# A convolution layer: GpSimd's diagonals behind the boundary's residual in short pieces, and a weight slab split during the taps

## The reference

```python
for i in range(DEPTH):
    kind, j = i % N_MIXERS, i // N_MIXERS
    a = rms_norm(h, mix_norm_pre[i])
    if kind == 0:
        m = dilated_attention_mixer(a, positions, attn_w_qkv[j], attn_w_o[j])
    elif kind == 1:
        m = short_conv_mixer(a, sc_w_in[j], sc_w_conv[j], sc_w_out[j])
    else:
        m = conformer_conv_mixer(a, cc_w_pw1[j], cc_b_pw1[j], cc_w_dw[j], cc_b_dw[j],
                                 cc_ln_g[j], cc_ln_b[j], cc_w_pw2[j], cc_b_pw2[j])
    h = h + rms_norm(m, mix_norm_post[i])
    f = conv_ffn(rms_norm(h, ffn_norm_pre[i]), ffn_w_in[i], ffn_w_conv[i], ffn_w_out[i])
    h = h + rms_norm(f, ffn_norm_post[i])
```

```python
def conformer_conv_mixer(x, w_pw1, b_pw1, w_dw, b_dw, ln_g, ln_b, w_pw2, b_pw2):
    a, g = jnp.split(x @ w_pw1 + b_pw1, 2, axis=-1)
    h = a * jax.nn.sigmoid(g)
    h = causal_dwconv(h, w_dw) + b_dw
    h = jax.nn.silu(layer_norm(h, ln_g, ln_b))
    return h @ w_pw2 + b_pw2
```

## Time and profile before

| | |
|---|---|
| median of 3 runs | 2284.12 us (2284.03 to 2288.83) |
| profiled execution | 2280.8 us, span of its profile 2278.9 us |
| PE busy | 2190.1 us |
| DVE busy | 1516.2 us |
| ACT busy | 1010.2 us |
| POOL busy | 461.5 us |
| end of layer 1's FFN on PE | 816.35 us |
| taps of layer 2 on PE | 884.25 to 925.9 us |
| output projection of layer 2 | 938.44 to 967.34 us |

### The profile page before, as it was taken

The page is one execution under the profiler, slowest core; times in us unless marked ns, Lnnn a source line. Parts: engine busy times, 40 slices in busy tenths (PEclk is TensorE's granted clock), DMA queues, the critical chain, the costliest instruction groups (busy, mean ns, idle before and its releaser), DMA issues.

```text
span 2278.9 us, 43583 instructions
## 1 busy us (share of the span) xinstructions
PE 2190.1 (96%) x16355; PEld 2004.7 (88%) x16355; DVE 1516.2 (67%) x2436; ACT 1010.2 (44%) x1355; POOL 461.5 (20%) x492
## 2 busy tenths in 40 slices
PE   6999999999999989999999999999999999989999
PEld 5998779978899868699889987799789999869999
DVE  6874868847688577388578848688465545645553
ACT  4334555534455433455443345555353342444342
POOL 2220005500145140035212200055013200100330
PEclk9999999999999989999999999999999999899999
DMA  5555135555545543245555551355545556103554
GB/s 170 184 184 184 38 127 175 185 192 165 192 163 185 178 130 121 69 162 184 180 167 187 185 190 41 109 177 184 190 153 166 175 175 189 43 1 130 184 187 145
DMA packets 299894, 350.28 MB, mean 154 GB/s; under 512 B 7494, under 2 KB 254940, under 8 KB 299804
## 3 DMA queue, kind: packets, MB, share of 16 engines
q1 hardware_dynamic: 298082, 347.07, 46.0%
q10 hardware_dynamic: 1466, 1.80, 0.2%
q0 software_dynamic: 256, 0.17, 0.0%
HBM read 346.34 MB, written 2.68 MB: 153 GB/s over the span
## 4 chain that ended last, share of the span: by engine, by line
PE 85%; DVE 9%; ACT 4%; issue 1%; DMA 1%; SPq 0%; ACTq 0%; DVEq 0%
PE ps L1980 25%; PE ps L1982 25%; PE ps L1981 24%; DVE w_lo L1461 3%; ACT w_hi L1092 2%; PE ps L2310 2%; PE ps L2281 1%; PE ps L2257 1%; DVE res L1583 1%; PE ps L2268 1%; DVE scaled_out L1577 1%; DVE a_lo L1487 1%; PE ps L930 1%; PE ps L2251 1%; DVE hstat L1520 1%
## 5 line engine op out<-in xcount | busy, mean ns | idle before, releaser
L1461 DVE TENSOR_TENSOR w_lo<-raw,w_hi 128x2048 fp32r<-128x2048 f32 (+2 forms) x328 | 744.4, 2270 | 534.4 <-ACT w_hi L1092 534.4
L1980 PE MATMUL ps<-a_hi,w_hi 128*128 128x256 f32 (+1 forms) x3352 | 953.5, 284 | 15.5 <-DVE a_lo L1487 7.6
L1981 PE MATMUL ps<-a_lo,w_hi 128*128 128x256 f32 (+1 forms) x3352 | 948.3, 283 | 0.0
L1982 PE MATMUL ps<-a_hi,w_lo 128*128 128x256 f32 (+1 forms) x3352 | 948.1, 283 | 0.0
L1092 ACT CAST w_hi<-raw 128x2048 fp32r<-128x2048 f32 (+2 forms) x328 | 613.4, 1871 | 626.7 <-PE ps L1982 603.7
L1980 PEld LDWEIGHTS ps<-a_hi,w_hi 128*128 128x128 f32 x3352 | 635.4, 190 | 20.3 <-DVE w_lo L1461 14.4
L1982 PEld LDWEIGHTS ps<-a_hi,w_lo 128*128 128x128 f32 x3352 | 635.8, 190 | 0.0
L1981 PEld LDWEIGHTS ps<-a_lo,w_hi 128*128 128x128 f32 x3352 | 632.7, 189 | 0.1
L1908 POOL TENSOR_TENSOR hs<-sg,cv 128x256 f32<-128x256 f32 x88 | 65.4, 743 | 734.4 <-DVE cv L1745 734.4
L1915 POOL CAST hid_hi<-hs 128x256 f32 (+3 forms) x132 | 140.2, 1062 | 329.1 <-DVE hs L1791 314.9
L1980 PE MATMUL ps<-w_hi,hid_hi 128*128 128x512 f32 x480 | 190.4, 397 | 10.7 <-DVE w_lo L1461 10.4
(11 more groups left out here) (277 smaller groups left out, 2462.0 us busy)
## 6 DMA issues: line engine op xcount, KB each, us to landing
raw<-in_ffn_w_in_dram SPq DMA_DIRECT2D x88, 1024.0 KB, 5.0
raw<-in_attn_w_qkv_dram SPq DMA_DIRECT2D x72, 1024.0 KB, 4.9
raw<-in_ffn_w_out_dram SPq DMA_DIRECT2D x32, 1024.0 KB, 5.0
raw<-in_ffn_w_gate_dram SPq DMA_DIRECT2D x22, 1024.0 KB, 5.1
raw<-in_ffn_w_up_dram SPq DMA_DIRECT2D x22, 1024.0 KB, 5.2
raw<-in_ffn_w_down_dram SPq DMA_DIRECT2D x16, 896.0 KB, 4.7
raw<-in_ffn_w_out_dram SPq DMA_DIRECT2D x16, 768.0 KB, 4.2
raw<-in_sc_w_in_dram SPq DMA_DIRECT2D x12, 1024.0 KB, 5.1
```

Of the source, the lines that this page charges most:

```text
L1461: dve.tensor_tensor(slab_view(w_lo, ph, j, j % 2), slab_view(raw, ph, j, j % 2), slab_view(w_hi, ph, j, j % 2).bitcast(F32), ALU.subtract) ...
L1980: pe.matmul(o, wh, xh, start=start, stop=False)
L1981: pe.matmul(o, wh, xl, start=False, stop=False)
L1982: return pe.matmul(o, wl, xh, start=False, stop=stop)
```

## The change

GpSimd now also waits, before its first diagonal, for `h_ready` of all residual additions so far, which includes the four of the boundary in front of `cc_in`. Each group's diagonals are made in four instructions (8, 8, 8 and 7 taps) instead of one; the semaphore is raised by the last.

The second slab of the convolution layer's output projection is split in `cc_mid`: its high split stands on ACT before the drains, its low split on DVE behind the taps and in front of the additions. In `out`, when the phase before is `cc_mid`, the splits begin with slab 2.

```diff
--- before.py
+++ after.py
@@ -1231,7 +1231,7 @@
                         act.activation(ostd[:, t:t + 1], osum[:, 2 + t:3 + t], ACT.Sqrt, bias=obias[:, t:t + 1],
                                        scale=1.0 / D).then_inc(post_std, 1)
 
-                    for j in range(1, ph.spb):
+                    for j in range(2 if ph.prior.kind == "cc_mid" else 1, ph.spb):
                         split_hi(ph, 0, j)
                     split_ahead(ph, 0, True)
                     square(0)
@@ -1326,6 +1326,7 @@
                         act.copy(work[HD:P, k, 0:SEQ], ps[0:HD, even + 1, 0:SEQ]).then_inc(cc_drained, 1)
 
                     load_table(act, ACT.Sqrt)
+                    split_hi(ph.next, 0, 1)
                     for t in range(len(CC_PE)):
                         drain(t)
 
@@ -1854,6 +1855,7 @@
                             dve.scalar_tensor_tensor(out=cacc[:, k, :], in0=gpad[:, k, bass.ds(j, SEQ)],
                                                      scalar=par[:, bass.ds(j * KD + (w0 + k), 1)], in1=cacc[:, k, :],
                                                      op0=ALU.mult, op1=ALU.add).then_inc(cc_tap, 1)
+                    split_lo(ph.next, 0, 1)
                     for t, k in enumerate(CC_PE):
                         dve.wait_ge(cc_drained, t + 1)
                         dve.tensor_tensor(cacc[:, k, :], cacc[:, k, :], work[:, k, 0:SEQ], ALU.add).then_inc(cc_added, 1)
@@ -1923,10 +1925,15 @@
                     pool.wait_ge(fold_ready, 1)
                     pool.wait_ge(par_ready, 2)
                     pool.wait_ge(tile_done, B["t"])
+                    pool.wait_ge(h_ready, 4 * B["post"])
                     for t in range(len(CC_PE)):
                         taps = par[:, w0:w0 + TAPS * KD].rearrange("p (j k) -> p j k", k=KD)[:, :, CC_PE[t]:CC_PE[t] + 1]
-                        pool.tensor_tensor(diag[:, t, :, :], fold[:].rearrange("p (a c) -> p a c", a=1).to_broadcast([P, TAPS, HD]),
-                                           taps.to_broadcast([P, TAPS, HD]), ALU.mult).then_inc(diag_ready, 1)
+                        for j0 in range(0, TAPS, 8):
+                            jn = min(8, TAPS - j0)
+                            op = pool.tensor_tensor(diag[:, t, j0:j0 + jn, :],
+                                                    fold[:].rearrange("p (a c) -> p a c", a=1).to_broadcast([P, jn, HD]),
+                                                    taps[:, j0:j0 + jn, :].to_broadcast([P, jn, HD]), ALU.mult)
+                        op.then_inc(diag_ready, 1)
 
                 elif ph.kind == "sc_b":
                     for k in range(KD):
```

## The result

The changed kernel takes 2270.73 us (median of 6 runs, 2267.63 to 2278.95); the kernel before took 2287.3 us in its runs beside it (6 runs, 2284.03 to 2288.83). The ratio is 0.9942, 95% interval 0.9926 to 0.9958: 13.3 us faster (0.0058 x 2287), between 9.6 and 16.9. The forecast was 16.1 us. The median lies in the forecast range; the execution that was profiled, 2278.95 us with a span of 2277.0, does not.

The account below looks back on a forecast made before the run. PE, busy 96% of the span, was taken as the bound, its waits for residual additions (10.0 us) and a low split (4.4) recoverable. 9.7 + 6.4 = 16.1 us off 2284.12 gave 2268.0, range 2263.5 to 2273.5.

Parts of the forecast that it names:

- part two: Output projection: splitting the second slab during the taps removes PE's wait and its slow clock, 6.4 us, bounds 3.6 and 6.6.
- The split's cover: Convolution taps: the moved high split (1.9 us, ACT) and low split (2.29 us, DVE) are hidden behind PE's taps.
- the third slab's slack: Output projection: the third slab is split at 948.6, PE wants it at 949.8, slack 1.2 us.
- Part one: Boundary before cc_in: diagonals begun behind the residual, in pieces, free the four additions; 9.7 us, bounds 6.8 to 12.4.
- boundary without GpSimd, from scaled_out: From scaled_out's start to the first matmul on the second slab, built from undisturbed boundaries; saves 12.44 us.
- pair L1531: Two single-column DVE operations at the boundary (L1530 before) wait for GpSimd pieces: 1.65 us together, at most 2.5.
- low split of the second slab: First iteration's second slab at the boundary: its DVE low split waits for a piece, 0.55 us, 0 to 1.26.
- spread L1554: Two DVE operations spreading the row factors at the boundary (L1553 before) take no lock and cost nothing.
- low splits in cc_in: Low splits of iterations 1 and 2 held by pieces beyond their slack: 0.5 us, bounds 0 and 1.8.
- My rival for it: Boundary: the spread is locked too, two further pieces, 1.7 us, giving 2269.7, with long pieces 2273; chance 0.09.
- The clock rival: Boundary: PE's clock falls after time without work before the first transposes, bounded by 2.8 us, giving 2270.8; chance 0.10.
- two slacks of 0.6 and 0.2: In cc_in, the splits of 852.82 and 858.94 are done 0.6 and 0.2 us before PE needs their slabs.

Follow-up runs that it names:

- after_again: The changed kernel, unchanged, run and profiled once more: ratio 0.9955 to the kernel before, median of 8 runs 2274.78 us.
- pass_filler: Changed kernel with diagonals starting behind the first pass over k, pieces of four taps, and 20 filler matmuls instead of 7 at this boundary: ratio 0.993 to before.
- late_whole: Changed kernel with each group's diagonals in one instruction again, still begun behind the residual: ratio 1.0003 to the kernel before.
- spread_act: Changed kernel with this boundary's row factors spread by ScalarE instead of VectorE's tensor_scalar: ratio 0.9917 to the kernel before, median 2265.95 us.

## Why the prediction was right or wrong

**Right in the sign, in what each part takes away, and in part two's size.** 6.4 us were forecast and 5.3 to 6.6 measured against the two profiles of before. The split's cover, the order of the queues and the third slab's slack were as argued.

**Part one was mis-sized: 9.7 forecast, 6.9 to 7.9 measured in the changed kernel, 6.0 alone.** My bounds for it were 6.8 to 12.4. That 6.9 lies inside them is luck: two of the terms below stood at nothing in the sum and had no bound there, and were made up for by a pair and a low split that stayed well under their own bounds of 2.5 and 1.3. Term by term, after and after_again:

| term | forecast | measured |
|---|---|---|
| boundary without GpSimd, from scaled_out | 14.51 | 14.51 (pass_filler) |
| pair L1531 | 1.65 | 1.27, 1.01 |
| low split of the second slab | 0.55 | 0.48, 0.49 |
| spread L1554 | 0 | 1.63, 1.62 |
| PE late at the lower clock | 0 | about 1.1, 0.3 (the remainder) |
| low splits in cc_in | 0.5 | 1.1, 1.1 |

**The step that failed** is the one that costed the spread at nothing "by the row". I had two lines of tensor_scalar and took 0.95 ns an element from them. With 1.6 us the spread is the largest of the lost terms that I had at nothing. The two lines are not alike: L1849 multiplies and adds, with two per-partition scalars, L1553 only multiplies. The row to compare with stood in the groups by line and form of before:

```profile
L1715 DVE TENSOR_SCALAR prob<-prob,cols 128x512 f32<-128x512 f32 x64 | 31.1, 487 | 2.2
```

512 elements in 487 ns against 128 in 284 is 0.53 ns an element, about half of what I had read off. The Trainium skill, "SBUF — State Buffer", section "Who interferes with whom", which says that such an operation can enter a two-port mode and take the lock it shares with GpSimd, is borne out: late_whole shows the wait (6.23 us instead of 0.48), and spread_act that the boundary is shorter without it. My rival for it gave 0.55 + 1.1 = 1.7, and 1.6 was measured; it deserved far more than 0.09. A page's statement about exactly this operation weighed more than a slope through two unlike rows.

**The clock rival came on top**, not instead. I bounded it by 2.8 us and gave it 0.10; in the kernels with short pieces that keep 7 fillers the granted clock of the 12 us behind scaled_out was 0.72 to 0.86, and what no VectorE wait explains of the boundary is 0.3 to 1.1. That the clock is the cause rests on pass_filler, one profile, in which the remainder is nothing at a clock of 1.00. scaled_out begins between 0.9 and 3.7 us behind PE's first filler from one execution to the next, and both profiles of before had 1.0: one execution's landing time made PE's idle time look short.

**cc_in** gave back 1.1, not 0.5. Its bounds, 0 to 1.8, held. Two slips of arithmetic change nothing: the share beyond the first slack is 0.11 to 0.12 by my own rule, not 0.14, and the upper end of the range, 2273.5, was set just under the 2273.7 of the joined bounds. I had counted two slacks of 0.6 and 0.2; the profile after shows splits held by 0.3 to 0.8 us, PE's waits of 0.6 in all, and part of the 1.1 is not in any wait that the profile lists.

**What I said of start against pieces was wrong.** "The start frees the additions; the pieces only keep what is left small": the pieces alone give 6.3 us, the start alone loses 3.5. In the forecast's own terms: with whole diagonals I had the pair at up to 3.59 + 3.59 and it took 5.14, but I never added the spread and the low split to it. The waits don't go away with a later start, they move to the next operations that share the lock, and those were as much on the chain as the additions.

What stays open: the remainder in cc_in, and why the slab ahead of the boundary lands so differently from one execution to the next. A start of the diagonals in which cc_in too is free of them wasn't tried.

## What to carry to other kernels

Where GpSimd works beside VectorE, list every VectorE operation on the critical chain that reads two tensors from SBUF or is a single-input tensor_scalar within SBUF, and price each at up to one GpSimd instruction's length; then cut that length before you move the start. A move alone only chooses which operations wait. Compare stretches between fixed points of the program when single executions scatter by more than the effect, and take a second profile of before: a transfer's landing time in one execution is no constant.

## What the runs showed that I had not expected

- GpSimd's lock comes back quickly: pieces of 512 elements take 1060 ns, of 256 elements 620 ns, so a cut in four costs GpSimd little (eighteen pieces of 1.06 and six of 0.95 make 24.8 us, six whole diagonals of 3.58 make 21.5; with VectorE's holds they take 32.0 and 23.5). Wherever a VectorE operation stood waiting in the timelines read here, it got in before the next piece.
- After 4.9 us of idle PE ran its fillers at the lower level (granted clock 0.64 in 821 to 827); with 0.9 us of idle in its place the same stretch ran at 1.00, and the boundary was 0.25 us shorter than with the same pieces and 7 fillers, in an execution in which PE was idle for 2.2.
- The granted clock in the second block, which no kernel here touches, differs between executions (0.83 and 0.74 in 1950 to 1990), and with it the time by several us.
